# Chunk stage of a gated delta rule: the output norm's mean squares with tokens on partitions

## The chip, the cores and the metric

The kernel is one program on one core of a Trainium2 chip. Its engines are PE (TensorE, the matrix products), DVE (VectorE), ACT (ScalarE), POOL (GpSimd) and SP (SyncE, which issues the transfers); each has its own queue of instructions, and they meet through semaphores. The metric is the time of one execution on the device in microseconds (us), the median of several.

## What is computed

One layer of a hybrid decoder for 2048 prompt tokens and 8 sample tokens. The change touches the prompt part of the gated delta rule, above all the norm of its output:

```python
def rmsnorm(x, g):
    xf = x.astype(jnp.float32)
    y = xf * lax.rsqrt(jnp.mean(xf * xf, axis=-1, keepdims=True) + RMS_EPS)
    return (y * g.astype(jnp.float32)).astype(x.dtype)
...
    a_mat = lower + jnp.eye(CHUNK, dtype=jnp.float32)
    u = lax.linalg.triangular_solve(a_mat, vc * bc[..., None], left_side=True, lower=True)
    w = lax.linalg.triangular_solve(a_mat, kb * jnp.exp(gc)[..., None], left_side=True, lower=True)
...
    def step(state, xs):
        u_i, w_i, q_i, k_i, a_i, gl_i = xs
        v_new = u_i - jnp.einsum('bhcd,bhde->bhce', w_i, state)
        o_i = jnp.einsum('bhcd,bhde->bhce', q_i, state) + jnp.einsum('bhij,bhje->bhie', a_i, v_new)
        state = state * gl_i[..., None, None] + jnp.einsum('bhcd,bhce->bhde', k_i, v_new)
        return state, o_i
...
        o_dn, new_delta = gated_delta_chunked(q, k, v, beta, g)
    o_dn = rmsnorm(o_dn.astype(x.dtype), g_dn_out) * jax.nn.silu(z_dn.reshape(B, S, DN_HEADS, DN_DV))
```

There are 4 heads of width 128. The norm is over the 128 channels of one token and one head: 2048 x 4 roots and reciprocals in all.

## The kernel before

The program runs stage after stage. The stage in question, `delta_and_attention`, takes the prompt in 16 chunks (`NC`) of 128 tokens, one after the other, since each needs the state `S_` that the one before left. Beside the delta rule it runs the dilated attention of the same tokens, cut into 12 steps a chunk plus two trailing slots; the calls `slot(c, par, j)` on PE, ACT and DVE put the attention's work between the parts of the delta rule. The order is written out by hand, engine by engine: each engine has its own `chunk`, and the semaphores alone tie them together. PE runs chunks 0, 1, 14 and 15 straight and chunks 2 to 13 in a loop of two chunks a turn.

One chunk goes like this. At its head DVE copies the last attention output, takes the reciprocal of the key and query norms (`rr`, 128x8), scales `kn` and `qn`, and adds the bias to the first scores (`slot` 0: `pb_s`); ACT takes their exponential, and PE turns it (L955). PE forms the decays' rows in bank 3 (`gbc`), later the Gram matrices in the same bank, and DVE multiplies them out into `L` and `M`. POOL makes `kbg` and `kdec` from `kn`, waits for `L`, and cuts it into six masked pieces `B`. Then the triangular matrix is inverted by halving in `LEVELS` = 7 levels: at each level PE forms Z = B XTh (the first product, which waits for DVE's update `xt_sub` of XTh), runs a slot of the attention, then forms the XT product and the X product; DVE subtracts the XT product from XTh (L1210, at levels 1 to 4) and the X product from X (L1224). At the end PE applies the inverse, forms the new values, the output `o` of the chunk in bank 2 with channels on partitions and tokens along the row, and the state's update.

The output's norm comes last. ACT squares the output into `osq` and keeps a copy `o_raw`. PE multiplies `osq` by `ones_mean`, a 128x128 tile of 1/128, into bank 3 (L1082): every partition then holds the mean square of every token, 128x512. ACT takes the root into `orr` (L883), 128x512, in the same chunk. DVE takes the reciprocal one chunk later, one head (128x128) behind the XTh update of each of the levels 1 to 4 (`invert`, L1156), and at level 5 scales the kept output by gain and reciprocal (`finish`, L1163). POOL multiplies by the gate (L769), and SP stores. PE's next use of bank 3 is the next chunk's `gbc` product, which waits for the root (`oroot_done`).

Of the kernel before, what the change touches and what calls it, by code (L numbers as in the profile page):

```python
# [27 lines left out]
P = 128  # L28
# [506 lines left out]
def heads(tile):  # L535
    return tile.rearrange("p (h j) -> p h j", h=HEADS)


def per_head(col):

    return col.rearrange("p (h o) -> p h o", o=1).broadcast_to([P, HEADS, P])
# [12 lines left out]
def delta_and_attention(nc, t):  # L554
# [13 lines left out]
    with ExitStack() as ctx:  # L568
# [19 lines left out]
        rr = sbuf("pb_rr", [P, 8], F32)  # L588
        coef = sbuf("pb_coef", [P, HEADS], F32)
        betag = sbuf("pb_betag", [P, NC, HEADS], F32)  # L590
        kn, kbg, kdec, qn, vb, knT, qnT, gbc, gd, E, egr, XT, U, WT, vnew, S_, intra, qdec, osq, orr, o, o_raw = (
            sbuf("pb_" + n, [P, C4], F32) for n in
            "kn kbg kdec qn vb knT qnT gbc gd E egr XT U WT vnew S intra qdec osq orr o o_raw".split())
        L, L21, M, X, XTh_, Y, Z = (sbuf("pb_" + n, [P, H4], F32) for n in "L L21 M X XTh Y Z".split())
        B = sbuf("pb_B", [P, IN_HALF, H4], F32)
        gain = sbuf("pb_gain", [P, 1], F32)
        eps = sbuf("pb_eps", [P, 1], F32)
        ones_mean = sbuf("pb_ones", [P, P], F32)
# [28 lines left out]
        rate_loaded = sem("pb_rate_loaded")  # L627
        gain_loaded = sem("pb_gain_loaded")
        beta_steps = sem("pb_beta_steps")
        block = ctx.enter_context(nc.Block())  # L630

        def const_tile(n):
# [6 lines left out]
        def bank(n):  # L639
            return ps[:, n, :]  # L640
# [104 lines left out]
        @block.gpsimd  # L745
        def _(pool):
            pool.memset(ones_mean[:, :], 1.0 / DK).then_inc(consts_set, 1)
            pool.memset(eps[:, :], EPS).then_inc(consts_set, 1)
            pool.memset(S_[:, :], 0.0).then_inc(consts_set, 1)
            pool.memset(XT[:, :], 0.0).then_inc(consts_set, 1)  # L750
            pool.memset(ones[:, :], 1.0).then_inc(consts_set, 1)
            for v in range(2):
                pool.memset(qkv[v][:, 1, 4 * P:8 * P], 0.0).then_inc(consts_set, 1)
                pool.memset(vtok[v][:, 1, :], 0.0).then_inc(consts_set, 1)
                pool.memset(bias[v][:, 0, :].rearrange("p (h k) -> p h k", h=AH)[:, :, 0:P], -BIG).then_inc(consts_set, 1)
            pool.wait_ge(consts_set, 11)
            pool.wait_ge(const_loaded, 32)
            def cc(tile, c):

                return tile[:, bass.ds(c, 1), :].rearrange("p o h -> p (o h)")  # L760

            def beta_of(c):
                return cc(beta, c).rearrange("p (h o) -> p h o", o=1).broadcast_to([P, HEADS, HALF_CH])

            def finish(c):

                pool.wait_ge(o1_done, c + 1)
                pool.wait_ge(z_loaded, c * 16 + 16)
                pool.tensor_tensor(o[:, :], o[:, :], zg[:, :], ALU.mult).then_inc(out_done, 1)  # L769

            def chunk(c, first=False):
                pool.tensor_tensor(heads(gbc[:, :]), all_heads(ones[:, :]), per_head(cc(g, c)), ALU.mult).then_inc(gbc_done, 1)
                pool.wait_ge(k_scaled, c + 1)
                pool.wait_ge(s_upd, c + 1)
                pool.tensor_tensor(heads(kbg[:, :]), heads(kn[:, :]), per_head(cc(betag, c)), ALU.mult)
                pool.tensor_tensor(heads(kdec[:, :]), heads(kn[:, :]), per_head(cc(ekd, c)), ALU.mult).then_inc(k_side_done, 1)
                pool.wait_ge(l_done, c + 1)
                for level in range(IN_HALF):
                    pool.tensor_tensor(in_half(B[:, level, :]), in_half(L[:, :]), all_heads_half(half_tile(level)),
                                       ALU.mult).then_inc(mask_done, 1)  # L780
                pool.wait_ge(m_done, c + 1)
                pool.tensor_tensor(in_half(L21[:, :]), in_half(M[:, :]), beta_of(c), ALU.mult).then_inc(mask_done, 1)
                if not first:
                    finish(c - 1)

            pool.wait_ge(gcol_done, 3)
            pool.wait_ge(betag_done, 1)
            chunk(0, True)
            with pool.Fori(1, NC) as c:
                chunk(c)  # L790
            finish(NC - 1)

        @block.scalar
        def _(act):
# [49 lines left out]
            def chunk(c, par, first=False, more=True):  # L844
# [35 lines left out]
                if more:  # L880
                    roots(c + 1)
                act.wait_ge(msq_done, c + 1)
                act.activation(orr[:, :], bank(3), ACT.Sqrt, bias=eps[:, 0:1]).then_inc(oroot_done, 1)  # L883
                slot(c, par, 13)

            square(0, 0, True)
# [14 lines left out]
        def _(pe):  # L901
# [79 lines left out]
            def turn_raw(c, n):  # L981
# [3 lines left out]
                    m = pe.transpose(col(bank(n), h), raw[:, 4 - 4 * n + h, :], ident)  # L985
                m.then_inc(kq_raw_turned, 1)

            def chunk(c, par, more=True, begun=False):
                if not begun:
                    slot(c, par, 0)  # L990
# [33 lines left out]
                for level in range(1, LEVELS):  # L1024
                    pe.wait_ge(mask_done, c * LEVELS + (level + 1))
                    pe.wait_ge(xt_sub, c * LEVELS + level)
                    pe.sem_inc(halves_begun, 1)
                    if level < IN_HALF:
                        m = in_halves(half_bank(0), lambda h: hcol(B[:, level, :], h), lambda h: hcol(XTh, h))
                    else:  # L1030
                        for h in range(HEADS):
                            m = pe.matmul(hcol(half_bank(0), h)[TOP], hcol(L21[:, :], h)[BOTTOM], col(XT[:, :], h)[BOTTOM, BOTTOM],
                                          start=True, stop=True)
                    m.then_inc(z_done, 1)
                    slot(c, par, level + 3)
                    pe.wait_ge(z_copied, c * (LEVELS - 1) + level)
                    pe.wait_ge(x_sub, c * (LEVELS - 1) + level)
                    pe.sem_inc(halves_begun, 1)
                    if level < IN_HALF:
                        m = in_halves(half_bank(1), lambda h: hcol(X[:, :], h), lambda h: hcol(Z[:, :], h))  # L1040
                    else:
                        for h in range(HEADS):
                            m = pe.matmul(hcol(half_bank(1), h)[TOP], hcol(X[:, :], h)[TOP], hcol(Y[:, :], h)[TOP],
                                          start=True, stop=True)
                    m.then_inc(xt_done, 1)
                    if level < IN_HALF:
                        if level == 1:
                            pe.wait_ge(i1_done, c + 1)
                            pe.sem_inc(halves_begun, 1)
                        in_halves(half_bank(2), lambda h: hcol(Z[:, :], h), lambda h: hcol(X[:, :], h)).then_inc(x_done, 1)  # L1050
                pe.wait_ge(xt_sub, c * LEVELS + LEVELS)
                pe.wait_ge(k_side_done, c + 1)
                for h in range(HEADS):
# [6 lines left out]
                if more:  # L1060
                    turn_raw(c + 1, 0)
                pe.wait_ge(w_copied, c + 1)
                for h in range(HEADS):
                    m = pe.matmul(col(bank(3), h), col(WT[:, :], h), col(S_[:, :], h), start=True, stop=True)
                m.then_inc(p1_done, 1)
# [13 lines left out]
                slot(c, par, 12)  # L1079
                pe.wait_ge(osq_done, c + 1)  # L1080
                pe.wait_ge(s_upd, c + 2)
                pe.matmul(bank(3), ones_mean[:, :], osq[:, :], start=True, stop=True).then_inc(msq_done, 1)  # L1082
                slot(c, par, 13)

            turn_raw(0, 0)
# [11 lines left out]
                chunk(2 * j + 1, 1)  # L1097
            chunk(NC - 2, 0)
            chunk(NC - 1, 1, False)

        @block.vector
        def _(dve):
# [47 lines left out]
                    dve.wait_ge(exp_done, c * STEPS + (j - 1))  # L1150
                    dve.tensor_copy(uo[v][:, 0:AH * HD], bank(OUTPUT)).then_inc(o_copied, 1)

            def invert(c, h):

                dve.wait_ge(oroot_done, c + 2)
                dve.reciprocal(col(orr[:, :], h), col(orr[:, :], h)).then_inc(orr_done, 1)  # L1156

            def finish(c):

                dve.wait_ge(orr_done, c * HEADS + HEADS)  # L1160
                dve.wait_ge(o_kept, c + 2)
                dve.wait_ge(o_free, c + 1)
                dve.scalar_tensor_tensor(o[:, :], o_raw[:, :], gain[:, 0:1], orr[:, :], ALU.mult, ALU.mult).then_inc(o1_done, 1)  # L1163

            def chunk(c, par, jj, first=False):
                def cc(tile):
# [8 lines left out]
                dve.tensor_tensor(heads(kn[:, :]), heads(bank(0)), per_head(rr[:, 0:4]), ALU.mult).then_inc(k_scaled, 1)  # L1175
                dve.wait_ge(coef_steps, c * 2 + 2)
                dve.tensor_tensor(heads(qn[:, :]), heads(bank(1)), per_head(coef[:, :]), ALU.mult).then_inc(q_scaled, 1)
                slot(c, par, jj, 0)
                dve.wait_ge(rows_done, c + 1)
                dve.tensor_tensor(heads(gd[:, :]), heads(bank(3)), per_head(cc(gc)), ALU.subtract).then_inc(g_diff_done, 1)  # L1180
# [25 lines left out]
                for level in range(1, LEVELS):  # L1206
# [8 lines left out]
                    else:  # L1215
                        m = dve.tensor_scalar(heads(XT[:, :])[TOP, :, BOTTOM], in_half(half_bank(1))[TOP], -1.0, None, ALU.mult)
                    m.then_inc(xt_sub, 1)
                    if level <= HEADS and not first:
                        invert(c - 1, level - 1)
                    if level == HEADS + 1 and not first:  # L1220
                        finish(c - 1)
                    if level < IN_HALF:
# [18 lines left out]
            with dve.Fori(1, NC // 2) as jj:  # L1241
                chunk(2 * jj, 0, jj)
                chunk(2 * jj + 1, 1, jj)
            for h in range(HEADS):
                invert(NC - 1, h)
            finish(NC - 1)


# [2131 lines left out]
```

## Time and profile before

| what | us |
|---|---|
| median of 3 runs | 3580.09 (3578.22 to 3580.46) |
| the profiled execution, its own time | 3580.37 |
| its span, first to last instruction | 3578.6 |
| the 16 chunks, from the first head to the last store | about 814 to 1616 |
| busy over the span: PE / DVE / ACT / POOL | 92% / 63% / 41% / 40% |
| busy from 862 to 1609 us, 15 chunks: PE / DVE / ACT / POOL | 652 / 504 / 467 / 152 of 747 |

Busy time tells how much work an engine has, not what ends a step. That is read from the waits: a row of waits names the instruction that could not start, the instruction that released it, the time lost in total, how often, and the longest. A row of a time line gives start, duration, engine, line of the code, operation, output and inputs, and in brackets how long the engine had stood idle before it and who ended that. Rows of the same kind that follow one another are merged, with their number behind the x. A float32 product of the code leaves two records on PE. PEclk is the granted clock of PE as a share of 2.4 GHz.

### The profile page before, as it was taken

How to read it: one execution, taken by the hardware profiler on the slowest of the kernel's cores; microseconds unless marked ns; L12 is line 12 of the kernel's file. 1: busy time of each engine (PE TensorE's matmuls, PEld its weight loads, DVE VectorE, ACT ScalarE, POOL GpSimd, SP SyncE). 2: the span in 40 equal slices, each digit the busy share in tenths (PEclk: the TensorE clock that was granted, in tenths of full speed). 3: DMA queues.
4: the chain of work that ended last, by engine and by line, in shares of the span. 5: the costliest groups of instructions: out<-in, count | busy, mean ns of one | idle time of the engine just before them, and what ended most of it. 6: DMA issues, size and time to landing. Idle time of an engine off the chain costs nothing. (4 is left out here: it accounts for less than half of the span.)

```text
span 3578.6 us, 64445 instructions
## 1 busy us (share of the span) xinstructions
PE 3282.7 (92%) x25026; PEld 3106.3 (87%) x25026; DVE 2270.9 (63%) x2876; ACT 1474.9 (41%) x3046; POOL 1420.9 (40%) x855
## 2 busy tenths in 40 slices
PE   8999999878888888886978999999999899999997
PEld 7899999847777777775977999999999899999997
DVE  6554122266666666667859999999988344334665
ACT  5111122136666566652324444454444343433332
POOL 3111111002211222112306988988887345555232
PEclk9999999969999999997989999999999999999998
DMA  3224244375333333316443553654433456465221
GB/s 119 78 72 77 94 164 164 134 228 141 94 100 85 87 98 91 95 54 192 140 146 132 180 193 115 204 177 146 157 115 99 160 173 199 160 203 181 93 84 68
DMA packets 304821, 473.49 MB, mean 132 GB/s; under 512 B 62830, under 2 KB 250414, under 8 KB 287232
## 3 DMA queue, kind: packets, MB, share of 16 engines
q1 hardware_dynamic: 304584, 470.21, 41.6%
q8 instruction: 163, 2.67, 0.3%
q14 instruction: 74, 0.61, 0.1%
HBM read 342.08 MB, written 161.50 MB: 141 GB/s over the span
## 5 line engine op out<-in xcount | busy, mean ns | idle before, releaser
L78 PE MATMUL gu_ps<-gu_xhi,gu_whi 128*128 128x344 f32 x1848 | 598.2, 324 | 18.5 <-DVE gu_xlo L2558 13.5
L80 PE MATMUL gu_ps<-gu_xlo,gu_whi 128*128 128x344 f32 x1848 | 594.1, 321 | 0.0
L79 PE MATMUL gu_ps<-gu_xhi,gu_wlo 128*128 128x344 f32 x1848 | 590.6, 320 | 0.0
L2399 POOL TENSOR_TENSOR gu_wlo<-gu_wsum,gu_whi 128x512 fp32r<-128x512 f32 x264 | 419.1, 1600 | 95.1 <-ACT gu_whi L2425 95.1
L78 PE MATMUL pa_proj<-pa_h_hi,pa_whi 128*128 128x412 f32 x1160 | 408.3, 352 | 24.8 <-DVE pa_h_lo L409 16.6
L79 PE MATMUL pa_proj<-pa_h_hi,pa_wlo 128*128 128x412 f32 x1160 | 408.0, 352 | 0.0
L80 PE MATMUL pa_proj<-pa_h_lo,pa_whi 128*128 128x412 f32 x1160 | 406.8, 351 | 0.0
L78 PEld LDWEIGHTS gu_ps<-gu_xhi,gu_whi 128*128 128x128 f32 x1848 | 349.4, 189 | 23.1 <-DVE gu_xlo L2558 12.4
L2902 POOL TENSOR_TENSOR pe_wlo<-down_w,pe_whi 128x1408 fp32r<-128x1408 f32 x76 | 255.8, 3375 | 255.4 <-ACT pe_whi L2937 255.2
L79 PEld LDWEIGHTS gu_ps<-gu_xhi,gu_wlo 128*128 128x128 f32 x1848 | 349.9, 189 | 0.4
L80 PEld LDWEIGHTS gu_ps<-gu_xlo,gu_whi 128*128 128x128 f32 x1848 | 349.1, 189 | 0.0
L2399 POOL TENSOR_TENSOR gu_wlo<-gu_w,gu_whi 128x512 fp32r<-128x512 f32 x198 | 320.1, 1625 | 67.4 <-ACT gu_whi L2425 67.4
L78 PE MATMUL pe_prod<-pe_ahi,pe_whi 128*128 128x412 f32 x880 | 310.9, 353 | 19.9 <-POOL pe_wlo L2902 10.9
L79 PE MATMUL pe_prod<-pe_ahi,pe_wlo 128*128 128x412 f32 x880 | 308.8, 351 | 0.0
L80 PE MATMUL pe_prod<-pe_alo,pe_whi 128*128 128x412 f32 x880 | 308.5, 351 | 0.0
L252 POOL TENSOR_TENSOR pa_wlo<-pa_w,pa_whi 128x1024 fp32r<-128x1024 f32 x29 | 87.3, 3009 | 512.7 <-ACT pa_whi L277 512.7
L2425 ACT ACTIVATE gu_whi<-gu_wsum 128x512 fp32r<-128x512 f32 x264 | 165.2, 626 | 300.4 <-DVE gu_wsum L2568 134.6
L3157 DVE TENSOR_TENSOR pe_acc<-pe_acc,pe_sq 128x412 f32<-128x412 f32 x35 | 70.0, 2000 | 296.3 <-ACT pe_sq L2960 296.2
L78 PEld LDWEIGHTS pa_proj<-pa_h_hi,pa_whi 128*128 128x128 f32 x1160 | 219.4, 189 | 27.4 <-issue 25.9
L472 DVE TENSOR_TENSOR pa_work<-pa_proj,pa_rstd 128x412 f32<-128x412 f32 (+1 forms) x85 | 49.7, 586 | 296.2 <-PE pa_proj L80 294.2
L2937 ACT ACTIVATE pe_whi<-down_w 128x1408 fp32r<-128x1408 f32 x80 | 109.8, 1381 | 275.8 <-DMA down_w<-in_w_down 255.8
L79 PEld LDWEIGHTS pa_proj<-pa_h_hi,pa_wlo 128*128 128x128 f32 x1160 | 219.4, 189 | 2.0 <-issue 0.8
(396 smaller groups left out, 7585.8 us busy)
## 6 DMA issues: line engine op xcount, KB each, us to landing
gu_w<-in_w_gate_up SPq DMA_DIRECT2D x66, 1024.0 KB, 5.6
down_w<-in_w_down SPq DMA_DIRECT2D x78, 704.0 KB, 4.2
scratch_at<-pa_work SPq DMA_DIRECT2D x24, 1024.0 KB, 5.6
pb_qkv<-scratch_at SPq DMA_DIRECT2D x32, 768.0 KB, 6.5
scratch_a<-gu_row SPq DMA_DIRECT2D x110, 172.0 KB, 5.6
out_new_cache_k<-in_cache_k SPq DMA_DIRECT2D x8, 2046.0 KB, 11.4
out_new_cache_v<-in_cache_v SPq DMA_DIRECT2D x8, 2046.0 KB, 11.5
pa_w<-in_w_in SPq DMA_DIRECT2D x29, 512.0 KB, 5.7
```

What stands on the lines that cost most here:

```text
L78: pe.matmul(out, w_hi, a_hi, start=first, stop=False)
L79: pe.matmul(out, w_lo, a_hi, start=False, stop=False)
L80: return pe.matmul(out, w_hi, a_lo, start=False, stop=last)
L252: pool.tensor_tensor(w_lo[:, par, :], w_raw[:, par, :], w_hi[:, par, :].bitcast(F32), ALU.subtract).then_inc(w_lo_done, 1)
L472: dve.tensor_tensor(into[0:parts, block_cols(b)], ps[0:parts, b, 0:TB], rstd[0:parts, block_cols(b)], ALU.mult).then_inc(evacuated, 1)
L2399: pool.tensor_tensor(w_lo[:, i, :], w_piece(W_PIECES[i], par), w_hi[:, i, :].bitcast(F32), ALU.subtract).then_inc(w_lo_done, 1)
L2425: act.activation(w_hi[:, i, :], w_piece(part, par), ACT.Copy).then_inc(w_hi_done, 1)
L2902: pool.tensor_tensor(w_lo[:, q, :], w_raw[:, q % 2, :], w_hi[:, q, :].bitcast(F32), ALU.subtract).then_inc(w_lo_done, 1)
L2937: act.activation(w_hi[:, q, :], w_raw[:, half, :], ACT.Copy).then_inc(w_hi_done, 1)
L3157: dve.tensor_tensor(acc[:, :], acc[:, :], sq[:, j % 2, :], ALU.add).then_inc(sums_done, 1)
```

## The change

The mean squares are formed with tokens on partitions. Instead of one product with `ones_mean` as weights, PE multiplies, head by head, with `osq` as weights and two columns of `ones_mean` as the moving operand: bank 3 then holds, per head, two equal columns with one number a token. ACT takes the root of 8 columns, DVE the reciprocal of 8 columns, once, at the head of the next chunk between `qn` and the first score step. To bring the numbers back along the rows, POOL multiplies the identity by them into `rdiag` (128x512, a diagonal a head), behind `kdec` and ahead of the masks, and PE multiplies `rdiag` by a tile of ones into bank 3, behind the X product of level 2. DVE's `finish` at level 5 reads bank 3 in place of `orr`. The four reciprocals in the levels are gone. Three waits are added on PE (the diagonal done; `m_done`, the last reader of bank 3; and `o1_done` ahead of the next product into bank 3), one on ACT (the diagonal has read `orr`), two on POOL.

```diff
+        orr = sbuf("pb_orr", [P, 2 * HEADS], F32)
...
 # POOL
+            def spread_roots(c):
+                pool.wait_ge(orr_done, c + 1)
+                pool.wait_ge(spread_done, c)
+                each = orr[:, 0:2 * HEADS:2].rearrange("p (h o) -> p h o", o=1).broadcast_to([P, HEADS, P])
+                pool.tensor_tensor(heads(rdiag[:, :]), all_heads(const_tile(C_IDENT)), each, ALU.mult).then_inc(diag_done, 1)
...
                 pool.tensor_tensor(heads(kdec[:, :]), heads(kn[:, :]), per_head(cc(ekd, c)), ALU.mult).then_inc(k_side_done, 1)
+                if not first:
+                    spread_roots(c - 1)
                 pool.wait_ge(l_done, c + 1)
...
 # ACT
                 act.wait_ge(msq_done, c + 1)
-                act.activation(orr[:, :], bank(3), ACT.Sqrt, bias=eps[:, 0:1]).then_inc(oroot_done, 1)
+                if not first:
+                    act.wait_ge(diag_done, c)
+                act.activation(orr[:, :], bank(3)[:, 0:2 * HEADS], ACT.Sqrt, bias=eps[:, 0:1]).then_inc(oroot_done, 1)
...
 # PE
+            def spread_roots(c):
+                pe.wait_ge(diag_done, c + 1)
+                pe.matmul(bank(3), ones[:, :], rdiag[:, :], start=True, stop=True).then_inc(spread_done, 1)
...
+                    if level == 2 and not begun:
+                        pe.wait_ge(m_done, c + 1)
+                        spread_roots(c - 1)
...
                 pe.wait_ge(w_copied, c + 1)
+                if not begun:
+                    pe.wait_ge(o1_done, c)
...
-                pe.matmul(bank(3), ones_mean[:, :], osq[:, :], start=True, stop=True).then_inc(msq_done, 1)
+                for h in range(HEADS):
+                    m = pe.matmul(bank(3)[:, 2 * h:2 * h + 2], col(osq[:, :], h), ones_mean[:, 0:2], start=True, stop=True)
+                m.then_inc(msq_done, 1)
...
             chunk(NC - 1, 1, False)
+            pe.wait_ge(oroot_done, NC + 1)
+            spread_roots(NC - 1)
...
 # DVE
-            def invert(c, h):
+            def invert(c):
                 dve.wait_ge(oroot_done, c + 2)
-                dve.reciprocal(col(orr[:, :], h), col(orr[:, :], h)).then_inc(orr_done, 1)
+                dve.reciprocal(orr[:, :], orr[:, :]).then_inc(orr_done, 1)
...
-                dve.wait_ge(orr_done, c * HEADS + HEADS)
+                dve.wait_ge(spread_done, c + 1)
...
-                dve.scalar_tensor_tensor(o[:, :], o_raw[:, :], gain[:, 0:1], orr[:, :], ALU.mult, ALU.mult).then_inc(o1_done, 1)
+                dve.scalar_tensor_tensor(o[:, :], o_raw[:, :], gain[:, 0:1], bank(3), ALU.mult, ALU.mult).then_inc(o1_done, 1)
...
                 dve.tensor_tensor(heads(qn[:, :]), heads(bank(1)), per_head(coef[:, :]), ALU.mult).then_inc(q_scaled, 1)
+                if not first:
+                    invert(c - 1)
                 slot(c, par, jj, 0)
...
-                    if level <= HEADS and not first:
-                        invert(c - 1, level - 1)
...
-            for h in range(HEADS):
-                invert(NC - 1, h)
+            invert(NC - 1)
             finish(NC - 1)
```

How the instructions stand on PE between levels 2 and 3 of a chunk of the loop, before (`pb_Z,pb_X` is the XT product, `pb_X,pb_Z` the X product, `pb_XTh,pb_B` the Z product of the next level):

```order
L955 MATMUL pb_ps<-pb_const,pb_e 128x128 x4
L1036 REGISTER_ALU
L914 MATMUL pb_ps<-pb_Z,pb_X 64x64 x8
L914 MATMUL pb_ps<-pb_X,pb_Z 64x64 x8
L1025 REGISTER_ALU
L914 MATMUL pb_ps<-pb_XTh,pb_B 64x64 x8
```

and after, where the line numbers are those of the changed kernel:

```order
L969 MATMUL pb_ps<-pb_const,pb_e 128x128 x4
L1054 REGISTER_ALU
L928 MATMUL pb_ps<-pb_Z,pb_X 64x64 x8
L928 MATMUL pb_ps<-pb_X,pb_Z 64x64 x8
L1004 MATMUL pb_ps<-pb_rdiag,pb_one 128x512
L1043 REGISTER_ALU
L928 MATMUL pb_ps<-pb_XTh,pb_B 64x64 x8
```

One wide product stands between the X product of level 2 and the Z product of level 3. At the end of the chunk, on PE before (L1077 is the state's update, L967 the attention's values, L1095 the end of the loop):

```order
L1077 MATMUL pb_ps<-pb_vnew,pb_kdec 128x128 x4
L967 MATMUL pb_ps<-pb_vtok,pb_eT 64x64 x4
L946 REGISTER_ALU
L955 MATMUL pb_ps<-pb_const,pb_e 128x128 x2
L1081 REGISTER_ALU
L1082 MATMUL pb_ps<-pb_osq,pb_ones 128x512
L967 MATMUL pb_ps<-pb_vtok,pb_eT 64x64 x4
```

and after:

```order
L1100 MATMUL pb_ps<-pb_vnew,pb_kdec 128x128 x4
L981 MATMUL pb_ps<-pb_vtok,pb_eT 64x64 x4
L960 REGISTER_ALU
L969 MATMUL pb_ps<-pb_const,pb_e 128x128 x2
L1104 REGISTER_ALU
L1106 MATMUL pb_ps<-pb_ones,pb_osq 128x2 x4
L981 MATMUL pb_ps<-pb_vtok,pb_eT 64x64 x4
```

The one wide product has become four narrow ones in the same place. On DVE at the head of a chunk, before (from the scaling of the keys to the first score step, L1141):

```order
L1174 REGISTER_ALU
L1175 TENSOR_TENSOR pb_kn<-pb_ps,pb_rr 128x512
L1177 TENSOR_TENSOR pb_qn<-pb_ps,pb_coef 128x512
L1131 ISA
L1133 ISA
L1141 SCALAR_TENSOR_TENSOR pb_s<-pb_ps,pb_bias 128x512
```

and after:

```order
L1201 REGISTER_ALU
L1202 TENSOR_TENSOR pb_kn<-pb_ps,pb_rr 128x512
L1204 TENSOR_TENSOR pb_qn<-pb_ps,pb_coef 128x512
L1183 RECIPROCAL pb_orr<-pb_orr 128x8
L1158 ISA
L1160 ISA
L1168 SCALAR_TENSOR_TENSOR pb_s<-pb_ps,pb_bias 128x512
```

The narrow reciprocal stands between `qn` and the first score step; the four wide ones of the levels are no longer in DVE's queue.

## Rows read from the trace of the kernel before

**Rows 1.** Waits of PE in 15 chunks (862 to 1612 us): total, times, longest.

```profile
PE pb_ps L955 <- ACT pb_e L840: 17.2, 13, 1.7
...
PE pb_ps L927 <- issue: 12.3, 5, 2.6
...
PE pb_ps L914 <- issue: 6.3, 15, 0.4
```

**Rows 2.** Waits of DVE in the same 15 chunks.

```profile
DVE pb_s L1141 <- PE pb_ps L940: 102.9, 73, 4.4
...
DVE pb_XTh L1210 <- PE pb_ps L914: 25.1, 45, 1.3
```

**Rows 3.** Time line of PE in one chunk, levels 2 and 3: start, duration.

```profile
1080.20 0.68 PE L914 MATMUL pb_ps<-pb_Z,pb_X 64*64 64x64 f32 x16
1080.72 0.63 PE L914 MATMUL pb_ps<-pb_X,pb_Z 64*64 64x64 f32 x16
1081.77 0.68 PE L914 MATMUL pb_ps<-pb_XTh,pb_B 64*64 64x64 f32 x16 [0.42 <-issue]
...
1084.67 0.68 PE L914 MATMUL pb_ps<-pb_Z,pb_X 64*64 64x64 f32 x16
```

**Rows 4.** Time line of DVE in the same levels.

```profile
1081.26 0.41 DVE L1210 TENSOR_TENSOR pb_XTh<-pb_XTh,pb_ps 128x256 f32<-128x256 f32 x1
1081.59 0.94 DVE L1156 RECIPROCAL pb_orr<-pb_orr 128x128 f32<-128x128 f32 x1
...
1085.40 0.42 DVE L1210 TENSOR_TENSOR pb_XTh<-pb_XTh,pb_ps 128x256 f32<-128x256 f32 x1 [0.42 <-PE pb_ps L914]
```

**Rows 5.** Time line of PE at the end of that chunk, which ends a loop turn.

```profile
1106.61 1.13 PE L1082 MATMUL pb_ps<-pb_osq,pb_ones 128*128 128x512 f32 x2 [0.75 <-DVE pb_S L1234]
1107.66 0.45 PE L967 MATMUL pb_ps<-pb_vtok,pb_eT 128*64 128x64 f32 x8
1110.71 0.65 PE L927 MATMUL pb_ps<-pb_const,pb_qkv 128*128 128x128 f32 x4 [2.59 <-issue]
```

**Rows 6.** Time line of DVE at a chunk's head, its narrow instructions.

```profile
1060.14 0.19 DVE L1171 RECIPROCAL pb_rr<-pb_rr 128x8 f32<-128x8 f32 x1
1060.36 0.17 DVE L1173 TENSOR_SCALAR pb_coef<-pb_rr 128x4 f32<-128x4 f32 x1
1060.46 0.69 DVE L1175 TENSOR_TENSOR pb_kn<-pb_ps,pb_rr 128x512 f32<-128x512 f32 x1
```

**Rows 7.** Narrow products of an earlier stage: ns min/median/max, first and last start us.

```profile
L1549 PE MATMUL sd_ps<-sd_kq,sd_state x64: 353/353/353, 744.6 to 758.0; 128*128 128x2 f32 x64
...
L1580 PE MATMUL sd_ps<-sd_ident,sa_keys x64: 246/246/349, 776.2 to 780.4; 8*128 8x2 f32 x64
```

**Rows 8.** Stretches: length, busy PE, PEld, DVE, ACT, POOL, PEclk, DMA share, GB/s.

```profile
744.60:758.00 13.40, 13.40 (x64) 13.40 (x65) 8.98 (x3) 0.00 (x0) 0.00 (x0) 0.50 1.07 316
776.20:780.70 4.50, 4.50 (x66) 4.48 (x64) 1.48 (x4) 0.59 (x1) 0.00 (x0) 0.95 0.00 0
1058.00:1064.30 6.30, 4.68 (x42) 3.33 (x42) 4.70 (x10) 4.90 (x10) 2.04 (x2) 1.00 0.16 54
```

**Rows 9.** Time line of PE: the first scores of two chunks.

```profile
1060.00 1.16 PE L940 MATMUL pb_ps<-pb_qkv 64*128 64x128 f32 x16
...
1111.29 2.08 PE L940 MATMUL pb_ps<-pb_qkv 64*128 64x128 f32 x16
```

**Rows 10.** Time line of POOL in one chunk.

```profile
1062.32 1.04 POOL L776 TENSOR_TENSOR pb_kdec<-pb_kn,pb_ekd 128x512 f32<-128x512 f32 x1
1070.47 5.34 POOL L779 TENSOR_TENSOR pb_B<-pb_L,pb_const 128x256 f32<-128x256 f32 x6 [7.11 <-DVE pb_L L1192]
```

**Rows 11.** Time line of all engines at the stage's end.

```profile
1610.41 3.38 DVE L1156 RECIPROCAL pb_orr<-pb_orr 128x128 f32<-128x128 f32 x4
...
1613.82 0.75 DVE L1163 SCALAR_TENSOR_TENSOR pb_o<-pb_o_raw,pb_gain,pb_orr 128x512 f32<-128x512 f32 x1
1614.65 1.26 POOL L769 TENSOR_TENSOR pb_o<-pb_o,pb_z 128x512 f32<-128x512 f32 x1 [16.82 <-DVE pb_o L1163]
```

More of the change, by code:

```diff
@@ L590, in delta_and_attention @@
         betag = sbuf("pb_betag", [P, NC, HEADS], F32)
-        kn, kbg, kdec, qn, vb, knT, qnT, gbc, gd, E, egr, XT, U, WT, vnew, S_, intra, qdec, osq, orr, o, o_raw = (
+        kn, kbg, kdec, qn, vb, knT, qnT, gbc, gd, E, egr, XT, U, WT, vnew, S_, intra, qdec, osq, rdiag, o, o_raw = (
             sbuf("pb_" + n, [P, C4], F32) for n in
-            "kn kbg kdec qn vb knT qnT gbc gd E egr XT U WT vnew S intra qdec osq orr o o_raw".split())
+            "kn kbg kdec qn vb knT qnT gbc gd E egr XT U WT vnew S intra qdec osq rdiag o o_raw".split())
         L, L21, M, X, XTh_, Y, Z = (sbuf("pb_" + n, [P, H4], F32) for n in "L L21 M X XTh Y Z".split())
         B = sbuf("pb_B", [P, IN_HALF, H4], F32)
+        orr = sbuf("pb_orr", [P, 2 * HEADS], F32)
         gain = sbuf("pb_gain", [P, 1], F32)
@@ L629, in delta_and_attention @@
         beta_steps = sem("pb_beta_steps")
+        diag_done = sem("pb_diag_done")
+        spread_done = sem("pb_spread_done")
         block = ctx.enter_context(nc.Block())
@@ L1099, in _ @@
             chunk(NC - 1, 1, False)
+            pe.wait_ge(oroot_done, NC + 1)
+            spread_roots(NC - 1)
         @block.vector
```

## The prediction

> **What bounds the kernel now.** The change touches one stage, the 16 chunks of the delta rule (about 814 to 1616 us of the span), so I read that stage alone. First the waits of PE over 15 chunks [rows 1]. They name what PE waits for and how often. At 15 entries per 15 chunks a wait is part of every chunk. PE's largest waits are at the head of a chunk: for ACT's exponentials (13 times, up to 1.7 us) and, at five loop ends, a stall of up to 2.6 us that no engine causes. In the halving levels only one wait of PE can have to do with the reciprocals that the change removes: L914 "issue", 6.3 us, 15 times, 0.42 us a chunk.
>
> Then the same view from DVE's side [rows 2]. In the levels DVE waits for PE: its update of XTh (L1210) waits 45 times in 15 chunks, that is at three of the four levels of that line. The score step (L1141) waits 102.9 us. So DVE, from which the work is taken, is mostly the engine that is early, and PE paces the levels.
>
> The time line of one chunk shows the exception [rows 3, 4]. At level 2 the copy of the attention output stands between, and the XTh update starts at 1081.26 with no wait of its own. PE begins the next level's products at 1081.77, 0.42 us late. At level 3, where DVE is early, the update comes 0.73 us after PE's XT product began (1084.67 to 1085.40). At level 2 it comes 1.06 us after (1080.20 to 1081.26). So the reciprocal of level 1, pushed in ahead, makes level 2's update 0.33 us late. The other three reciprocals cost nothing: the waits behind them are for PE.
>
> **The change part by part.** The four reciprocals of 128x128 go from DVE's levels (0.95 us each, 0.87 from start to start: 1081.59 to about 1082.45). By the above only 0.33 us of the 3.5 is on the path, and the new product takes that place.
>
> *The ones-product at level 2* is new on PE: one 128x512 float32 product, two records, of the same form as the mean-square product of before, which held PE from 1106.61 to 1107.66, 1.05 us [rows 5]. It stands behind level 2's X product and ahead of level 3's Z product. The X product begins at 1080.72 and needs 0.52 us (as the XT product before it, 1080.20 to 1080.72). So the ones-product begins at about 1081.24 and ends at 1082.29. Without the reciprocal XTh is updated by then (1080.93 plus the 0.51 us from its start to PE's next product is 1081.44), so the wait lies under the product and level 3 begins at 1082.29 instead of 1081.77: +0.52 us. From there to the chunk's end PE has no slack that could take it up; what waits for PE shifts with it. 15 chunks do this: 15 x 0.52 = +7.8 us.
>
> *The narrow mean squares* at the chunk's end: the 128x512 product becomes four products with osq as weights and two moving columns, eight records with eight full weight loads. This lies on the path: the attention values behind it (L967) release DVE's copy and with it the whole head of the next chunk. The trace has this very form once, at L1549 in an earlier stage: 64 records from 744.6 to 758.0, 13.4/63 = 0.213 us each, but all at a granted clock of 0.50 (1.2 GHz) [rows 7, 8]. At a chunk's end and head the clock is full (1.00) [rows 8]. Halved, an estimate, that is 0.106 us, eight are 0.85 us, and 1.05 - 0.85 saves 0.20. The bounds: nothing saved at all, and 0.52 saved by the other narrow row of the trace (L1580, 64 records of 8x2 with 8-row weights, 776.2 to 780.4 at a clock of 0.95, 4.2/63 = 0.067 us each, eight are 0.53). I take 0.20, since L1549 is the same form, and the clock the difference that the rows show. 15 x 0.20 = -3.0 us; the sixteenth is in the tail.
>
> *The narrow reciprocal* moves to the head of the chunk, between qn and score step 0 on DVE. The 128x8 reciprocal that stands there already takes 0.19 us, and the instruction behind it starts 0.22 us later when it needs the result; a 128x4 one takes 0.10 from start to start when it does not [rows 6]. I take 0.12 here, with bounds 0.10 and 0.22. Behind it stand the scores, their maximum, ACT's exponentials and PE's turn, which waits up to 1.7 us for exactly this chain [rows 1]; so it counts at the heads without a loop stall. At the five with one, DVE waits for late scores anyway and hides it. Its own wait, for ACT's root, is over: the root follows the mean squares, and three wide steps of DVE lie between. 10 x 0.12 = +1.2 us.
>
> *The diagonal* is one more POOL instruction of 128x512 behind kdec, with the same kind of operands as kdec (1.04 us). POOL then waits 7.11 us for L before the masks [rows 10]; the cover leaves 6 us. If the cover were gone, the masks would be late by 1.04. Costed at nothing, and so are the new waits: PE's for m_done and for the diagonal were met some 10 us and more before, that for o1_done lies two levels behind DVE's finish, ACT's guards a tile read long ago. The narrow root only shortens ACT.
>
> *The tail*, once: behind the last mean squares DVE now spends 3.41 us from the first reciprocal to the scaling (1610.41 to 1613.82) [rows 11]. After: a reciprocal of 0.19, the diagonal 1.04, the ones-product 1.05 and three hand-overs of about 0.1 (the scaling's to POOL took 0.08: 1613.82 + 0.75 to 1614.65) make 2.6. With the sixteenth saving of 0.20: -1.0 us.
>
> The sum is 7.8 - 3.0 + 1.2 - 1.0 = +5.0 us against the profiled execution's 3580.4 us (its span of 3578.6 and 1.8 around it). That execution lies 0.3 above the median of 3580.1, so the forecast is 3585.1.
>
> **The rivals.** *Cheap narrow products*, 3580.2. If a narrow product costs the 0.067 us of L1580 also with 128 rows of weights, each chunk's end saves 0.52 instead of 0.20, and the sum is 7.8 - 7.8 + 1.2 - 1.3 = -0.1. For it: both forms load 128 columns and stream two. Against it: L1549's spacing is three times L1580's, at a clock that is half. The Trainium skill, page "TensorE: Matmul & The Clock Gate", section "LDWEIGHTS (loading the stationary operand)", says that a load's time goes by its columns and not by its rows; by that L1580's 128 columns would price the new ones and this rival would be the sum. The two rows here, each with 128 columns, differ by more than the factor of the clock, so the trace does not bear the rule out; it keeps a chance of 0.14.
>
> *The gap stays*, 3593. This is the one that ends slower. The trace calls PE's 0.42 us at level 3 "issue" and no DVE wait. If it is not the late XTh but something between the semaphore and the issue, the ones-product does not cover it, and the whole 1.05 is added: 15 x 1.05 - 2.8 = +13. It decides from a cost of 0.66 us a chunk on (15 x 0.66 - 2.8 = 7.1), that is once more than 0.14 us of the gap is left. For it speaks only the label; against it the arithmetic above, where XTh's end (1081.26 + 0.41) and PE's start are 0.10 apart. 0.14.
>
> *The clock falls at more heads*, about 3603. After each of the loop stalls the clock drops, and the scores then took 2.08 us where another head took 1.16 [rows 9]. L1549's back-to-back narrow products ran for 13.4 us with the clock at 0.50 throughout [rows 8]. So a narrow product may not hold the clock up as a wide one does, and a chunk's end now has a wait, 0.85 us of narrow products and a short values step. Price: 0.92 us for the scores and, an estimate, as much again for what follows, at ten heads 18 us on top of the 5. Two such heads are nearly enough to leave "the same". Against it: the stretch is short, and the transposes and scores come directly behind it at those heads. The same page of the Trainium skill, in the section on the HAM clock gate, has the clock follow how busy PE has been; by that the narrow products, with PE busy all through, would hold it and this rival would be nil. In [rows 8] PE was busy all the 13.4 us and the clock stayed at 0.50, so the measurement speaks against the rule. 0.07.
>
> *DVE was the bound after all.* Then 15 x 3.4 us go and the time is near 3532. DVE's waits for PE in every level [rows 2] speak against it. A part of this, with the ones-product hidden in a wait I don't see, would give 15 x (-0.42) - 2.8 = -9, 3571. Together 0.05.
>
> **How the numbers follow.** Forecast 0.60, cheap products 0.14, gap stays 0.14, clock 0.07, DVE 0.05. About 0.2% (7.2 us) is what a measurement of this kernel can tell from no change. The forecast's own range, with the bounds of the narrow products and the reciprocal, goes from 3580 (the cheap products) to 3589 (nothing saved: 7.8 + 2.2 - 0.8 = 9.2); about a quarter of its 0.60 lies above 3587.3. So slower: 0.15 + 0.14 + 0.07 = 0.36; faster: 0.05; the same: 0.59. The range takes in the cheap products and the gap that stays: 3579.5 to 3593.5, which leaves out the clock and DVE.
>
> **What would show it.** Level 2 to 3: the time from the X product to the next Z product grows by 0.5 (1.05 if the gap stays), and L914's "issue" wait is gone. The mean squares hold PE for 0.85 (0.53 if cheap) before L967. DVE's waits grow by what the reciprocals took, and its busy time falls by some 55 us with no gain. POOL's diagonal ends before L is there. The granted clock at heads without a stall is 1.00 as before. The forecast is wrong if PE shows idle time at level 2 that the product fills, or if the chunk's period moves by something outside these three places.

## The result

Side by side on one chip the changed kernel took 3597.91 us (median of 6 runs, 3585.97 to 3601.70) against 3579.48 us: a ratio of 1.0047, interval 1.0032 to 1.0063. On a second chip it was 3597.59 against 3585.54 us, 1.0029 (1.0017 to 1.0041). So it is slower by 10 to 17 us by these ratios, and by 12 and 18 us between the medians. The forecast was +5.0 us, and the predicted range ended at 3593.5: the time lies above it.

The profiled execution of after is the one of 3585.97 us (span 3584.2), the fastest of its six. To compare parts I cut the stage on PE's time line, in every profile alike. A *head* runs from a chunk's mean squares to the Gram product of the next chunk (L1013 in before), a *body* from there to the product with kbg (L1054), an *end* from there to the mean squares. Sums in us over 16 bodies, 16 ends, and 15 heads, of which five follow a loop stall ("stall heads"); "long ends" are those in which the product with kbg takes over 1.3 us. "Before, again" and "after, again" are a second profile of each kernel.

| kernel | bodies (a typical one) | ten heads | five stall heads | ends (long ones) | sum |
|---|---|---|---|---|---|
| before | 455.9 (28.48) | 99.7 | 64.8 | 165.4 (2) | 785.8 |
| before, again | 456.0 (28.49) | 99.8 | 64.6 | 170.2 (5) | 790.5 |
| after | 464.8 (29.05) | 102.6 | 67.6 | 162.3 (0) | 797.3 |
| after, again | 464.6 (29.05) | 103.5 | 67.8 | 171.9 (6) | 807.8 |

The sum grew by 11.5 us from the first profile to the first and by 17.3 from the second to the second: bodies +8.7 to +8.9, ten heads +2.9 to +3.7, five stall heads +2.8 to +3.2. The rest is the long ends (-3.1 and +1.7), which every kernel with PE's old waits can have. The parts tell more than the spans here: outside them the same four executions took from 2786.9 to 2795.2 us (before 2792.8 and 2788.1, after 2786.9 and 2795.2), so that the first two spans differ by 5.6 us only.

The page of after, busy time of each engine, and the largest waits of PE in the same 15 chunks (total, times, longest), to be held against [rows 1]:

```profile
PE 3301.1 (92%) x25154; PEld 3123.9 (87%) x25154; DVE 2226.6 (62%) x2828; ACT 1468.7 (41%) x3046; POOL 1435.6 (40%) x871
```

```profile
PE pb_ps L969 <- ACT pb_e L852: 13.8, 11, 1.7
PE pb_ps L941 <- issue: 12.0, 5, 2.6
...
PE pb_ps L1106 <- DVE pb_S L1261: 11.6, 15, 0.8
...
PE pb_ps L1004 <- POOL pb_rdiag L778: 2.1, 1, 2.1
```

The "issue" wait at the levels' products is gone, as the ones-product fills it. Only one wait of PE names the diagonal, the one in the tail. DVE is 44.3 us less busy (2270.9 before) and waits longer: its score step waits 136.2 us for PE where [rows 2] had 102.9.

**The ones-product.** Time line of PE in after, levels 2 and 3 of the chunk of [rows 3], then that chunk's end, which answers to [rows 5] (start, duration, engine, line; in brackets the idle time before it):

```profile
1085.15 0.68 PE L928 MATMUL pb_ps<-pb_Z,pb_X 64*64 64x64 f32 x16
1085.67 0.63 PE L928 MATMUL pb_ps<-pb_X,pb_Z 64*64 64x64 f32 x16
1086.23 1.12 PE L1004 MATMUL pb_ps<-pb_rdiag,pb_one 128*128 128x512 f32 x2
1087.29 0.68 PE L928 MATMUL pb_ps<-pb_XTh,pb_B 64*64 64x64 f32 x16
...
1112.13 1.05 PE L1106 MATMUL pb_ps<-pb_ones,pb_osq 128*128 128x2 f32 x8 [0.75 <-DVE pb_S L1261]
1113.11 0.45 PE L981 MATMUL pb_ps<-pb_vtok,pb_eT 128*64 128x64 f32 x8
1115.92 1.11 PE L941 MATMUL pb_ps<-pb_const,pb_qkv 128*128 128x128 f32 x4 [2.35 <-issue]
```

From the X product to the next Z product it is now 1.62 us (1085.67 to 1087.29) where it was 1.05: +0.57. The narrow mean squares hold PE for 0.98 us (1112.13 to 1113.11) where the wide product held it for 1.05: only 0.07 is saved.

**The clock at a head without a loop stall.** Time line of PE in after, from the mean squares of one chunk into the head of the next:

```profile
960.10 1.05 PE L1106 MATMUL pb_ps<-pb_ones,pb_osq 128*128 128x2 f32 x8 [0.75 <-DVE pb_S L1261]
961.08 0.45 PE L981 MATMUL pb_ps<-pb_vtok,pb_eT 128*64 128x64 f32 x8
961.46 1.12 PE L941 MATMUL pb_ps<-pb_const,pb_qkv 128*128 128x128 f32 x4
962.51 2.08 PE L954 MATMUL pb_ps<-pb_qkv 64*128 64x128 f32 x16
964.52 1.30 PE L1012 MATMUL pb_ps<-pb_const,pb_gbc 128*128 128x128 f32 x8
...
967.29 0.65 PE L969 MATMUL pb_ps<-pb_const,pb_e 128*128 128x128 f32 x4 [1.03 <-ACT pb_e L852]
```

The same place in stretches of 1 us (length, busy PE with instructions, granted clock of PE, DMA share, GB/s):

```profile
960.00:961.00 1.00, 0.90 (x8) 1.00 0.00 0
961.00:962.00 1.00, 1.00 (x13) 0.71 0.05 16
962.00:963.00 1.00, 1.00 (x7) 0.50 0.00 0
963.00:964.00 1.00, 1.00 (x14) 0.50 0.66 264
964.00:965.00 1.00, 1.00 (x9) 0.58 0.02 6
965.00:966.00 1.00, 1.00 (x12) 1.00 0.00 0
```

PE is busy without a gap, yet from 961 to 965 the clock is at or near 0.50 (1.2 of 2.4 GHz). The scores take 2.08 us instead of 1.16, the transposes before them 1.12 instead of 0.65. PE's later wait for the exponentials takes up a part (1.03 us here). Three such heads are 10.84 to 11.01 us long; the heads of after whose clock holds are 9.87 to 10.00. There is a fourth head at which the clock falls, but 2.48 us behind the start of the mean squares where it was 1.04 to 1.33 at the three; it is 10.12 us long. So the fall costs less the later it comes. In before the clock falls at none of the ten, and all are 9.88 to 10.01.

### The profile page after: what moved, and what is told of

The parts are those of the page before. It is cut to its first block and busy times, and to the rows that moved or that the text cites. A ratio compares the mean times of both kernels' runs of the same rounds, so it can differ in the third digit from the quotient of the medians.

```text
span 3584.2 us, 64717 instructions
## 1 busy us (share of the span) xinstructions
PE 3301.1 (92%) x25154; PEld 3123.9 (87%) x25154; DVE 2226.6 (62%) x2828; ACT 1468.7 (41%) x3046; POOL 1435.6 (40%) x871
## 6 DMA issues: line engine op xcount, KB each, us to landing
out_new_cache_k<-in_cache_k SPq DMA_DIRECT2D x8, 2046.0 KB, 11.5
```

## The experiments

**After once more.**

> The changed kernel as it is, to see how its runs spread. Its profile showed three heads without a loop stall (chunks 3, 7, 11) that took 0.8 to 1.0 us longer, with the clock at 0.50 in them. If the clock is what makes the other runs of it 10 us and more longer than the profiled one, another profile shows other or more such heads, and the mean granted clock falls with the time. If the clock is not it, the heads without a stall stay at 10.0 us and the time is lost elsewhere.

3597.59 us against 3585.54, 1.0029 (1.0017 to 1.0041). The bodies agree with after's first profile within 0.2 us. Six of the ten heads are longer than 10.3 us, between 10.38 and 11.00, and at a seventh (10.14) the clock falls late. The mean granted clock over the span was 0.957 to 0.960 in these six executions, and 0.956 to 0.959 in the five on the first chip that were longer than the profiled one, which had 0.964. The loss is real, and the number of heads with a fallen clock differs from execution to execution.

**The four products with 128 moving columns instead of two.** After, with

```
-  m = pe.matmul(bank(3)[:, 2*h:2*h+2], col(osq[:, :], h), ones_mean[:, 0:2], ...)
+  m = pe.matmul(col(bank(3), h), col(osq[:, :], h), ones_mean[:, :], ...)
```

and the root reading two columns of each head's 128.

> The changed kernel with 128 moving columns of ones_mean in place of 2 in each of the four mean-square products; ACT's root reads two columns of each head. The products take as long as the narrow ones (eight records of 128 columns took 0.99 us elsewhere, the narrow ones 0.98). If the narrow products let the clock fall, all heads without a stall are at 10.0 us again, and the time is about 10 us under that of the changed kernel, near 3587. If the clock has nothing to do with them, the time is that of the changed kernel, near 3597.

3595.11 us against 3585.54, 1.0026 (1.0016 to 1.0037). Time line of PE at the head shown above, and the clock there in stretches:

```profile
964.23 1.16 PE L1106 MATMUL pb_ps<-pb_ones,pb_osq 128*128 128x128 f32 x8 [0.75 <-DVE pb_S L1261]
965.32 0.45 PE L981 MATMUL pb_ps<-pb_vtok,pb_eT 128*64 128x64 f32 x8
965.70 0.66 PE L941 MATMUL pb_ps<-pb_const,pb_qkv 128*128 128x128 f32 x4
966.28 1.16 PE L954 MATMUL pb_ps<-pb_qkv 64*128 64x128 f32 x16
...
970.68 0.65 PE L969 MATMUL pb_ps<-pb_const,pb_e 128*128 128x128 f32 x4 [1.71 <-ACT pb_e L852]
```

```profile
965.00:966.00 1.00, 1.00 (x15) 1.00 0.06 16
966.00:967.00 1.00, 1.00 (x16) 1.00 0.00 0
967.00:968.00 1.00, 1.00 (x13) 1.00 0.45 180
```

64 times as many columns cost 0.11 us (1.09 instead of 0.98), and the clock holds: the ten heads are all 9.98 to 10.11 us (100.8 in sum), the stall heads 64.4 instead of 67.6. By its heads the profile says that the narrowness makes the clock fall. The time near 3587 that was expected for this case was missed by 8 us: the ones-product with its 8.6 us stays in this kernel, and what the heads lost in the two profiles of after is 5.7 and 6.9 us, not 10. By the medians alone (2.5 us, of which 15 x 0.11 = 1.7 go back to the longer products) this run would not decide it.

**Each new product alone.** Two kernels from before. The first has only the narrow mean squares (the four products of after; the root is fed a scale of 0, so the norm is left out). The second has only one more 128x512 product at level 2, whose result is not read.

```
-  pe.matmul(bank(3), ones_mean[:, :], osq[:, :], ...).then_inc(msq_done, 1)
+  for h in range(HEADS):
+      m = pe.matmul(bank(3)[:, 2*h:2*h+2], col(osq[:, :], h), ones_mean[:, 0:2], ...)
+  m.then_inc(msq_done, 1)
```

> The kernel before with only the mean squares made narrow (four products with osq as weights and two moving columns); the wide root, the four reciprocals and the scaling stay, and the root's scale is 0, so that the norm's numbers are left out. If the narrow products let the clock fall, heads without a stall get 0.9 us longer in some chunks, and the time is 3 to 12 us above before. If not, each chunk's end is 0.07 us shorter and the time is 1 us under before.

```
+  if level == 2 and not begun:
+      pe.wait_ge(m_done, c + 1)
+      pe.matmul(bank(3), ones_mean[:, :], osq[:, :], start=True, stop=True)
```

> The kernel before with one more 128x512 product at level 2 (ones_mean by the last osq into bank 3, which nobody reads), and nothing else. Each of 15 chunks should be 0.57 us longer between the Gram products and the use of the inverse, 8.6 us in all, whatever the clock does at the heads; the heads stay at 10.0 us.

Narrow products alone: 3593.72 against 3585.54, 1.0020 (1.0011 to 1.0029). Ten heads 104.8 (six of them 10.59 to 10.98), stall heads 67.4, bodies 456.3. So a product that is itself 0.07 us shorter makes the kernel 8 us slower, by the profile 5.1 of it at the ten heads and 2.6 at the stall heads. The ones-product alone: 3594.73, 1.0026 (1.0016 to 1.0037). Bodies 465.2 (+0.57 a chunk with the reciprocals still in place), all ten heads 9.88 to 10.01, stall heads 63.5. The two costs are separate and of about the same size: +8.2 and +9.2 us. Added up they are more than the 12.1 us of after on this chip; the intervals leave room for that, and no run explains it otherwise. The clock of the executions that were not profiled says the same as the heads: on this chip its mean was 0.957 to 0.960 in all 17 executions with the two-column products (after, narrow products alone) and 0.961 to 0.965 in all 38 without (128 columns, ones-product alone, before).

**After without the ones-product**, its place taken by a bare signal (the scaling then reads what the mean squares left there), and before once more.

```
-  pe.matmul(bank(3), ones[:, :], rdiag[:, :], ...).then_inc(spread_done, 1)
+  pe.sem_inc(spread_done, 1)
```

> The changed kernel without the ones-product (a semaphore stands in its place, and the scaling reads what the bank holds, so the numbers are not brought along the rows). If the wait of 0.42 us before level 3 came from the reciprocal of level 1, it is gone here, and a chunk takes 28.06 us from the Gram products to the use of the inverse: 28.48 before, 29.05 with the product (1.05 less 0.06 that is lost to the hand-over). If the wait was of another kind, 28.48. The heads stay as in the changed kernel: some of those without a stall at 10.4 to 11.0, since the narrow products are still there.

> The kernel before, for a second profile of it. Heads without a stall at 9.9 to 10.0 in every chunk if only the narrow products let the clock fall there; the longer ends of chunks (11.7 in place of 10.15), of which the first profile had two and others up to five, are expected here too, two to five of them, since every kernel shows them.

3585.36 us, one run (before there: median 3579.84 of 21). A body takes 28.18 us (28.06 was expected): taking the reciprocals from the levels is worth 0.30 of the 0.42 us that PE waited there. Ten heads 102.4, stall heads 68.0, as in after. Before once more: 3580.41 us, second row of the table.

**The ones-product in waits that PE still has.** PE waits in level 6 of every chunk of before: 0.53 us ahead of L1032 and 0.51 ahead of L1054. In this version the ones-product is cut into two halves of 256 columns, one for each wait, the products have 128 columns, the scaling on DVE goes behind the last XT step, and the narrow reciprocal behind the second score step. A second version is the same with two columns.

```
-  if level == 2 and not begun:
+  if level == IN_HALF - 1 and not begun:
       pe.wait_ge(m_done, c + 1)
-      spread_roots(c - 1)
+      spread_roots(c - 1, 0)
+  if level == IN_HALF and not begun:
+      spread_roots(c - 1, 1)
```

> A version built on the findings: 128 moving columns in the mean squares, the ones-product cut into two halves of 256 columns that stand in PE's two waits of 0.53 and 0.51 us at level 6, the scaling behind the last update of XT, the narrow reciprocal behind score step 1, where DVE waits for PE. Expected: 28.1 to 28.2 us from Gram products to the use of the inverse, heads at 10.0 with no clock fall, 6 to 7 us less than before over the stage; and PE busy where it waited may spare some of the longer ends of chunks, up to 5 us more. If the halves don't fit the waits, 28.6 and no gain.

> The same version with two moving columns in the mean squares in place of 128. If these let the clock fall, some heads without a stall are at 10.4 to 11.0 and those with a stall 0.5 longer on the mean, together 5 to 7 us in a profile and 4 to 10 us in the median against the version with 128 columns. If the clock is blind to them, the two agree.

With 128 columns 3574.63 us against 3579.84, 0.9987 (0.9978 to 0.9996); with two columns 3581.45, 1.0002 (0.9993 to 1.0012). PE's time line of the first, the halves and the loop end behind them:

```profile
1090.60 0.63 PE L928 MATMUL pb_ps<-pb_X,pb_Z 64*64 64x64 f32 x16
1091.17 0.70 PE L1005 MATMUL pb_ps<-pb_rdiag,pb_one 128*128 128x256 f32 x2
1091.80 0.68 PE L1053 MATMUL pb_ps<-pb_XT,pb_L 64*64 64x64 f32 x8
...
1093.38 0.67 PE L1064 MATMUL pb_ps<-pb_Y,pb_X 64*64 64x64 f32 x8
1093.99 0.70 PE L1005 MATMUL pb_ps<-pb_rdiag,pb_one 128*128 128x256 f32 x2
1094.57 1.16 PE L1080 MATMUL pb_ps<-pb_XT,pb_kbg 128*128 128x128 f32 x8
...
1109.43 0.84 PE L941 MATMUL pb_ps<-pb_const,pb_qkv 128*128 128x128 f32 x4 [3.17 <-issue]
```

Each half lies where PE waited, and a body falls to 28.23 us, 0.25 under before. Between the two versions only the columns differ, and with them where ACT's root reads: ten heads 100.1 and 103.0 us, five of the narrow ones 10.39 to 10.98. With the stall heads (69.7 against 68.4) that is 4.2 us, where 5 to 7 were expected in a profile. This pair settles in medians what the first 128-column run left open: 6.8 us (3581.45 - 3574.63). The intervals against before just touch (0.9993 to 0.9996 is in both), but eight of the 11 executions with 128 columns were faster than the fastest with two, and the mean clock was 0.964 to 0.966 in all of them, 0.958 to 0.962 in all with two. Over all twelve profiles the clock falls at 30 of the 50 heads without a stall in the five with two columns, and at none of 70 in the seven with 128 or 512. The gain is smaller than the 6 to 7 us over the stage that were expected: the sum of the parts is 782.8, 3.0 and 7.7 under the two profiles of before, since the stall heads, 68.4 us, are longer than before's though the products are wide.

**Filled waits alone.** Neither profile of the pair had a long end. In before one looks like this (time line of PE, then stretches as above):

```profile
1395.32 0.65 PE L1032 MATMUL pb_ps<-pb_XT,pb_L 64*64 64x64 f32 x8 [0.53 <-issue]
...
1398.06 2.08 PE L1054 MATMUL pb_ps<-pb_XT,pb_kbg 128*128 128x128 f32 x8 [0.51 <-DVE pb_XT L1216]
1399.93 1.78 PE L1057 MATMUL pb_ps<-pb_vb,pb_XT 128*128 128x128 f32 x8
```

```profile
1397.00:1398.00 1.00, 0.55 (x8) 1.00 0.07 16
1398.00:1399.00 1.00, 0.94 (x4) 0.52 0.52 158
1399.00:1400.00 1.00, 1.00 (x7) 0.50 0.46 107
```

The clock falls right behind the two waits. So I added to before two 256-column products in these waits, whose results nobody reads, and ran the 128-column version again beside it.

```
+  if level == IN_HALF - 1 and not begun:
+      pe.wait_ge(m_done, c + 1)
+      pe.matmul(bank(3)[:, 0:2*P], ones_mean[:, :], osq[:, 0:2*P], ...)
+  if level == IN_HALF and not begun:
+      pe.matmul(bank(3)[:, 2*P:4*P], ones_mean[:, :], osq[:, 2*P:4*P], ...)
```

> The kernel before with two 256-column products added in the two waits of PE in level 6 (0.53 us at L1032, 0.51 us at L1054); what they compute is never read. Question: are the long chunk ends (the clock at 0.50 from the product with kbg, +1.6 us each, 0 to 6 of 16 in every profile with those waits, none in the two with the waits filled) caused by the waits? If they are: no long end in 16, the sum of the ends 162.3 us instead of 165 to 170, the bodies unchanged (28.48, at most 0.15 more each for what does not fit into the waits), and a time from 5 us below the kernel before to 1 above it, although the kernel does more work. If they are not: 2 to 6 long ends as before, and a time at or up to 3 us above the kernel before.

> The version with the halves at level 6 and 128 columns once more. If its earlier 5 us under the kernel before is real: 0.9987 within 0.001, no long end, bodies of 28.23 us. If it was chance: a ratio of 1.000 and 2 to 6 long ends. The five heads behind a loop stall took 68.4 us in its first profile against 64.8 in the kernel before; again 68 if that belongs to the version, 64 to 65 if not.

PE's time line of before with the fillers, where the waits were:

```profile
1398.14 0.70 PE L1053 MATMUL pb_ps<-pb_osq,pb_ones 128*128 128x256 f32 x2
1398.77 0.68 PE L1032 MATMUL pb_ps<-pb_XT,pb_L 64*64 64x64 f32 x8
...
1400.96 0.70 PE L1055 MATMUL pb_ps<-pb_osq,pb_ones 128*128 128x256 f32 x2
1401.54 1.16 PE L1059 MATMUL pb_ps<-pb_XT,pb_kbg 128*128 128x128 f32 x8
```

3578.35 us against 3581.95, 0.9991 (0.9982 to 1.0000), with no long end, ends 162.2 us in sum, heads as in before, bodies 456.9 (+0.06 each). More work, and if anything less time. Over all profiles: with the waits open, 32 long ends of 128, in seven of eight profiles; with them filled, none of 64 in four (chunk 0, where nothing is filled, has no long end in any profile). That the waits bring the fall is shown by the profiles; the time alone touches "no change". The version again: 3576.32 us, 0.9985 (0.9976 to 0.9994), bodies 28.23, no long end, stall heads 67.0. It is the fastest kernel here: faster than before in both measurements, by 0.13 and 0.15%.

## Why the prediction was wrong

- **The ones-product: right.** Predicted +0.52 a chunk, measured +0.57 (15 chunks: 8.6 of the 8.7 to 8.9 us on the bodies). The "gap stays" rival falls: the late XTh lies under the product. With the reciprocals still in the levels or without them, a body is the same 0.57 longer than before's, so what was freed on DVE is worth nothing while the product stands there. DVE's busy time fell by 44.3 us, not by some 55.
- **The narrow products: the term was mis-sized.** Predicted 0.85 us and -3.0 in sum, measured 0.98 and 15 x 0.07 = -1.0. The halving of L1549's 0.213 us to 0.106 was the step that failed: at full clock a record took 0.123 (0.98 / 8). "Cheap products" (0.067) falls too. The Trainium skill, page "TensorE: Matmul & The Clock Gate", section "LDWEIGHTS (loading the stationary operand)", prices a load by its columns, in ns their number over 1.2; worked out for 128 that is 107 ns, and 0.85 for eight, an estimate. The row has 0.98.
- **The narrow reciprocal: right in size, less on the path.** Predicted 0.12, measured 0.11 from start to start. A head got only 0.07 longer by it: where the clock holds, a typical head takes 10.11 us with the 128-column products in after's order and 10.04 in the level-6 version, where the reciprocal stands elsewhere. On the time line of DVE in after:

```profile
1066.54 0.19 DVE L1183 RECIPROCAL pb_orr<-pb_orr 128x8 f32<-128x8 f32 x1
1066.65 0.64 DVE L1168 SCALAR_TENSOR_TENSOR pb_s<-pb_ps,pb_bias 128x512 f32<-128x512 f32 x1
```

- **The diagonal: right**, hidden. POOL in after:

```profile
1068.19 1.04 POOL L778 TENSOR_TENSOR pb_rdiag<-pb_const,pb_orr 128x512 f32<-128x512 f32 x1
1075.42 5.35 POOL L790 TENSOR_TENSOR pb_B<-pb_L,pb_const 128x256 f32<-128x256 f32 x6 [6.18 <-DVE pb_L L1221]
```

- **The tail: wrong by 1 us.** Predicted -1.0, measured about 0 (last mean squares to store: 7.74 us before, 7.80 after). All engines of after, with the ones-product twice as long as I took it, at a granted clock of 0.50 (1623.9 to 1626.1) behind PE's wait:

```profile
1622.52 0.19 DVE L1183 RECIPROCAL pb_orr<-pb_orr 128x8 f32<-128x8 f32 x1
...
1623.99 2.05 PE L1004 MATMUL pb_ps<-pb_rdiag,pb_one 128*128 128x512 f32 x2 [2.12 <-POOL pb_rdiag L778]
...
1626.07 0.75 DVE L1190 SCALAR_TENSOR_TENSOR pb_o<-pb_o_raw,pb_gain,pb_ps 128x512 f32<-128x512 f32 x1 [3.35 <-PE pb_ps L1004]
```

- **The clock: the main failure.** I held "the clock falls at more heads" for a rival of 0.07, at ten heads or none. It happened at four and seven of the ten in the two profiles of after, at 0.2 to 1.1 us each (0.92 to 1.8 was my price), and I did not count the five stall heads at all, where before's clock falls too: there it cost another 2.8 to 3.2 us. My reason against it, that the stretch is short, fails at 961 us above. The row that spoke for it was before me: L1549's narrow products at a clock of 0.50 with PE busy all through [rows 8]. By itself that row does not single out the columns: from 729.2 to 742.2 us PE was as busy with products of 384 columns (33 rows of weights), and the clock was 0.50 as well. A better row stood in the same trace, unnoticed: the 64 two-column products of L1580 began at a clock of 1.00, and from 780.3 to 783.5 us, with PE busy all through, it was 0.50. The Trainium skill, page "TensorE: Matmul & The Clock Gate", section "Part 1: The HAM clock gate", has the clock go by how busy PE has been. That rule was weighed against [rows 8] and found wanting, yet the chance stayed small. The runs decide: equally busy, the two-column products let the clock fall and the 128-column ones do not. Whether they would without PE's wait of 0.75 us ahead of them, which both kernels have, no run here shows.

Two totals of the rivals do not follow from their terms, and nothing hangs on them: the cheap products' -0.1 gives 3580.0 and not 3580.2, and DVE as the bound, 15 x 3.4 us, gives 3529 and not 3532.

The sum with the measured terms, against before's heads and bodies: bodies +8.8, heads +3.3 (the reciprocal and the shorter products within it), stall heads +3.0, tail 0, about +15 us where I had +5.0. Some 6.6 us of it is the clock at the heads; without it the measured terms make 8.5 us (bodies 8.8, shorter products -1.0, reciprocal +0.7), which the range would have held. The two ratios say 10.4 us (0.0029 x 3585.5) and 16.8 (0.0047 x 3579.5).

Left open: how many of the other runs' microseconds are long ends and how many fallen heads, since only profiled executions show them one by one (after's other five runs on the first chip lay 10 to 16 us above the profiled one, at a lower mean clock); and why the stall heads of the level-6 version with 128 columns are 2 to 4 us longer than before's. The clock alone does not explain these: its mean over the five was 0.87 in that version's second profile (67.0 us) as in before's second (64.6).

## What to carry to other kernels

Before a product is made narrow because it is shorter, look what the clock does behind it: a saving of 0.07 us a chunk cost up to 1.1 us at a head, and 128 columns instead of two, for 0.11 us, took that loss away. A new product on the engine that paces the loop belongs into a wait that this engine really has at each turn (level 6 here, found in the waits of PE), not behind the step whose other engine the change relieves. Where a time line shows an instruction twice as long as its twin, read the granted clock there before looking for a wait.

## What was new about the hardware

- Two moving columns or 128 with full weights: 0.98 and 1.09 us for eight records at full clock, so the columns are nearly free. Behind the two the clock fell at 30 of 50 heads without a stall, behind 128 or 512 at none of 70, with PE equally busy.
- Two waits of PE of 0.5 us (L1032 and L1054), with products between them, were followed in 32 of 128 ends by a clock near 0.50. With the waits filled, by products whose results are read or not, this was gone in all 64 ends profiled.
